# One output projection in a hybrid decoder step: pairs of full row tiles by seven half-size products in place of eight

## What is computed

```python
branch_a = jnp.einsum('blv,vd->bld', o_r.astype(dt), w_ret_up)
...
branch_b = jnp.einsum('blv,vd->bld', o_d.astype(dt), w_dn_up)

merged = jax.nn.sigmoid(gate_a) * branch_a + jax.nn.sigmoid(gate_b) * branch_b
h = h + jnp.einsum('bld,de->ble', merged, w_out)

u = rmsnorm(h, norm_ffn)
grp_logits = (jnp.einsum('bld,dg->blg', u, w_router_group) + b_router_group).astype(f32)
...
exp_logits = (jnp.einsum('bld,de->ble', u, w_router_expert) + b_router_expert).astype(f32)
...
w_top = jax.nn.softmax(top_v, axis=-1) * p_grp
```

## Time and profile before

| | us |
|---|---|
| median of three runs | 884.6 |
| lowest, highest | 884.51, 887.13 |
| the profiled execution's own time | 886.13 |
| its span in the trace | 884.3 |

### The profile page before, as it was taken

The page is one execution under the profiler, slowest core; times in us unless marked ns, Lnnn a source line. Parts: engine busy times, 40 slices in busy tenths (PEclk is TensorE's granted clock), DMA queues, the critical chain, the costliest instruction groups (busy, mean ns, idle before and its releaser), DMA issues.

```text
span 884.3 us, 11837 instructions
## 1 busy us (share of the span) xinstructions
PE 862.4 (98%) x4657; PEld 558.2 (63%) x4657; DVE 363.5 (41%) x833; ACT 223.4 (25%) x476; POOL 153.5 (17%) x186
## 2 busy tenths in 40 slices
PE   9999999999999999999999999999999999999996
PEld 4546777887799876776777755455444444444452
DVE  3223565766556325566434542234311111104553
ACT  2211243274223211131011103120211111125554
POOL 0324320022243314200300340002000000003100
PEclk9999999999999999999999999999999999999998
DMA  9512342502020202334122235015999999785111
GB/s 365 186 76 91 127 133 99 149 1 103 1 98 3 96 2 67 135 126 132 65 126 95 97 126 210 24 45 218 389 373 370 360 378 348 298 310 172 59 49 47
DMA packets 19813, 135.98 MB, mean 154 GB/s; under 512 B 2512, under 2 KB 3024, under 8 KB 12592
## 3 DMA queue, kind: packets, MB, share of 16 engines
q1 hardware_dynamic: 12176, 103.28, 30.5%
q0 software_dynamic: 5424, 26.45, 8.5%
q10 hardware_dynamic: 2160, 5.51, 2.1%
HBM read 117.83 MB, written 21.60 MB: 158 GB/s over the span
## 4 chain that ended last, share of the span: by engine, by line
PE 87%; DVE 4%; ACT 4%; issue 2%; DMA 1%; POOLq 0%; POOL 0%; ACTq 0%; DVEq 0%
PE pair L718 15%; PE single L1200 12%; PE single L898 11%; PE pair L1108 7%; PE pair L1189 6%; PE pair L793 4%; PE pair L769 3%; PE pair L1302 3%; PE pair L919 3%; PE single L919 3%; PE single L1177 2%; PE pair L1240 2%; PE single L974 1%; PE single L996 1%; PE single L993 1%
## 5 line engine op out<-in xcount | busy, mean ns | idle before, releaser
L718 PE MATMUL pair<-mem 128*128 128x288 f32 x640 | 158.9, 408 | 0.0
L718 PEld LDWEIGHTS pair<-mem 128*128 128x128 f32 x640 | 120.3, 190 | 35.6 <-ACT mem L1323 2.1
L1200 PE MATMUL single<-mem 128*128 128x512 f32 x256 | 112.8, 593 | 1.4 <-DVE mem L2160 1.4
L898 PE MATMUL single<-mem 128*128 128x288 f32 x448 | 110.1, 407 | 0.2
L898 PEld LDWEIGHTS single<-mem 128*128 128x128 f32 x448 | 84.7, 190 | 25.8 <-issue 1.6
L1200 PEld LDWEIGHTS single<-mem 128*128 128x128 f32 x256 | 47.3, 190 | 54.7 <-issue 53.1
L1323 ACT ACTIVATE mem<-single 128x256 f32<-128x256 f32 (+5 forms) x113 | 46.5, 421 | 132.7 <-PE single L1117 51.0
L1323 ACT ACTIVATE mem<-pair 128x512 f32<-128x512 f32 (+5 forms) x83 | 36.6, 492 | 162.5 <-PE pair L718 63.1
L1108 PE MATMUL pair<-mem 128*128 128x512 f32 (+1 forms) x192 | 64.6, 527 | 0.5 <-DVE mem L2000 0.5
L2153 DVE SCALAR_TENSOR_TENSOR mem<-single,mem 128x256 f32<-128x256 f32 x16 | 7.7, 484 | 138.8 <-PE single L1200 126.3
L1302 PE MATMUL pair<-mem 128*128 128x512 f32 (+1 forms) x192 | 63.4, 524 | 0.9 <-DVE mem L2206 0.9
(11 more groups left out here) (385 smaller groups left out, 1111.9 us busy)
## 6 DMA issues: line engine op xcount, KB each, us to landing
mem<-in_w_gu SPq DMA_DIRECT2D x16, 2048.0 KB, 9.5
mem<-in_w_down SPq DMA_DIRECT2D x16, 1024.0 KB, 11.8
y_slots<-mem SPq DMA_DIRECT2D x16, 512.0 KB, 3.9
y_slots<-in_zeros POOLq DMA_DIRECT2D x8, 512.0 KB, 8.1
mem<-in_w_ga SPq DMA_DIRECT2D x2, 2048.0 KB, 8.5
mem<-in_w_gb SPq DMA_DIRECT2D x2, 2048.0 KB, 8.4
mem<-in_w_wo SPq DMA_DIRECT2D x2, 2048.0 KB, 8.4
mem<-in_w_pg SPq DMA_DIRECT2D x2, 2048.0 KB, 11.3
```

The costliest lines, as they stand in the source:

```text
L718: last = nc.tensor.matmul(pb[:, hf, 0:HALF], w(k), rhs[:, k, hf * HALF:(hf + 1) * HALF], start=(k == 0), stop=(k == kk - 1))
L898: last = nc.tensor.matmul(single[plan.buf[s]][:, 0:HALF], lhs[:, k, :], rhs[:, k, :], start=(k == 0 and j in (0, 1, 3, 4)), stop=(k == 3), ...
L1200: last = nc.tensor.matmul(single[3][:, :], xT[u % 2][:, k, :], w_gu[u][:, k, :], start=(k == 0), stop=(k == KD - 1))
```

## The change

The four full tiles go in pairs, (0, 1) and (2, 3). Of a pair, the two row tiles, the two halves of the 1024 features and the two halves of the 1024 output columns make eight half-size products of four matmuls. The change replaces them by seven products on sums and differences of rows and weights (`sx`, with `sh` for the first half of the seventh), in the same scheme of sums that the branch groups have. The half with index h holds the feature blocks 2h, 2h+1, 4+2h and 5+2h.

- Weights: four combinations `sum_w`. Two are made by VectorE in steps of 512 columns behind products 1 to 4 of each of the last two branch groups (`sxT` 0 and 1), two of 2048 columns ahead of the first pair (`sxT` 2 and 3).
- Rows: four combinations for each pair (`sxS`), 512 columns each, with one more add; those of the first pair behind the last branch group, those of the second among the first pair's products.
- Results: ScalarE copies the first product of a pair from its bank; VectorE forms two partial sums (`sxu`), adds them to the residual rows (`sxp`) and then adds the banks (`wo`), ten adds of 512 columns per pair where there were four.
- Order: tiles now pass the router as 1, 0, 3, 2, 4 and the small tile is projected last, its two halves cut into four steps (`wg`, `wo`, `wh`, `wo`) among the router steps of tiles 3 and 2. The router steps of tiles 1 and 0 stand among the second pair's products.
- SyncE loads expert 1's weights after the sixth product of pair 1, as two of the weight sums lie in its place. GpSimd stores the rows of tiles 1 and 3 after their first half, which is now the later one.

The core of the diff:

```diff
-ORDER = [0, 4, 1, 2, 3]
+ORDER = [1, 0, 3, 2, 4]
...
+                if r == q == 1 and 0 < j < 5:
+                    out += [("sxT", x, j - 1)]
                 if r == q == x == 0:
                     out += {0: [("nf", "oN", 0)], 1: [("nf", "oN", 1)], 2: [("nf", "oN", 2)], 3: [("nf", "oN", 3)]}.get(j, [])
+        return out
+
+    def wo_pair(p, early):
+
+        out = []
+        for j in range(7):
+            out += early[j] + [("sx", p, j)]
+            out += {1: [("sxp", p, 0), ("wo", 2 * p, 0)] + [("sxS", 1, i) for i in range(3) if p == 0], 3: [("sxu", p), ("sxp", p, 1), ("sxp", p, 2)],
+                    4: [("wo", 2 * p + 1, 1)], 5: [("wo", 2 * p + 1, 0)], 6: [("wo", 2 * p, 1)]}.get(j, [])
         return out
 
     for r in range(2):
         for g in range(4 * r, 4 * r + 4):
             s += fast_group(g)
         s += fast_pair(r, 0) + fast_pair(r, 1)
-    for i, t in enumerate(ORDER):
-        s += [("wo", t, 0)]
-        if i: s += [("x2b", ORDER[i - 1])]
-        if i >= 2: s += [("rank", ORDER[i - 2])]
-        if i: s += [("rt", ORDER[i - 1])]
-        s += [("wh", t)]
-        if i: s += [("rtT", ORDER[i - 1])]
-        s += [("x2a", t), ("sqa", t)]
-        if i >= 2: s += [("ids", ORDER[i - 2])]
-        if i == 3: s += [("ovp", 0)]
-        s += [("wo", t, 1)]
-    y, z = ORDER[3:]
-    s += [("idv", t) for t in ORDER[:2]] + [("x2b", z), ("rank", y), ("rt", z), ("rtT", z), ("ids", y)]
+    s += wo_pair(0, [[("sxS", 0, 0), ("sxS", 0, 1), ("sxT", 2, 0), ("sxS", 0, 2), ("sxT", 3, 0)], [], [], [], [], [], [("sh", 0)]])
+    x2 = lambda t: [("x2a", t), ("sqa", t)]
+    s += wo_pair(1, [x2(1) + [("x2b", 1)], x2(0) + [("rt", 1)], [("x2b", 0), ("rtT", 1)], [("rt", 0)], [("rtT", 0), ("rank", 1)],
+                     [("ids", 1), ("rank", 0), ("ovp", 0)], [("sh", 1), ("ids", 0)] + x2(3) + [("x2b", 3)]])
+    s += [("wg", 4), ("rt", 3)] + x2(2) + [("wo", 4, 0), ("rtT", 3), ("x2b", 2), ("wh", 4), ("rt", 2), ("wo", 4, 1)] + x2(4)
+    s += [("rank", 3), ("rtT", 2), ("x2b", 4), ("idv", 1), ("ids", 3), ("rank", 2), ("rt", 4), ("idv", 0), ("ids", 2), ("rtT", 4)]
+    z = 4
...
+            if k == "sx":
+                nmm += 1
+                self.mm[s], self.before[s] = nmm, None
+            if k == "wo" and s[1] == 4:
+                nmm += 1
+                self.mm[s] = nmm
+                self.buf[s], self.before[s] = s[2], (None, ("wo", 3, 0))[s[2]]
+                last[("pair", s[2])] = s
...
+        half_rows = lambda t, h: mT.rearrange("p (a h b) c -> p a h b c", a=2, h=2)[:, :, h, :, t * P:t * P + P]
+        half_w = lambda i, h: ring[(13 + i) % RING].rearrange("p (a h r) -> p a h r", a=2, h=2)[:, :, h, :]
+        sum_w = [view(at, 2, 1024) for at in (OR, slot(0), UT + 2048, slot(4))]
+        sum_rows = [[view(at + 512 * i, 2, 2, P) for i in range(4)] for at in (RINGO + 2048, SQ)]
+        wpart = [view(slot(24 + i), 512) for i in range(3)]
...
+        sx_bank = [pair[i // 2][:, i % 2, :] for i in (0, 1, 2, 0, 3, 2, 3)]
...
+            free[1] = ("sx", 1, 5)
...
+                elif k0 in ("sx", "sh"):
+                    p = s[1]
+                    j = 6 if k0 == "sh" else s[2]
+                    ta, tb = 2 * p, 2 * p + 1
+                    prev = [("uy", 1, 1, 1, 2), ("uy", 1, 1, 1, 1), ("uy", 1, 1, 1, 5), None, ("uy", 1, 1, 1, 6), None, ("wo", tb, 1)] if p == 0 else \
+                           [None, ("wo", 0, 0), ("wo", 1, 0), None, ("wo", 0, 1), None, ("wo", tb, 1)]
+                    if prev[j] is not None:
+                        ev_wait(pe, prev[j])
+                    if j == 0 and p == 1:
+                        pe.wait_ge(sem("sx_part"), 1)
+                    if j == 3:
+                        pe.wait_ge(sem("sx_p0"), p + 1)
+                    if j == 5:
+                        pe.wait_ge(sem("sx_part"), 2 * p + 2)
+                    w_at = {0: (0, 0), 1: (0, 1), 6: (1, 1)}.get(j)
+                    if w_at:
+                        chunk(("wo", 4, w_at[0]))
+                    else:
+                        pe.wait_ge(sem("sum_w"), {2: 4, 3: 9, 4: 8, 5: 10}[j])
+                    if j in (2, 3, 4, 6):
+                        pe.wait_ge(sem("sum_rows"), 3 * p + {2: 1, 3: 2, 4: 2, 6: 3}[j])
+                    wgt = half_w(*w_at) if w_at else sum_w[{2: 2, 3: 1, 4: 0, 5: 3}[j]]
+                    rows = {0: half_rows(ta, 0), 1: half_rows(ta, 1), 5: half_rows(tb, 1)}[j] if j in (0, 1, 5) else \
+                        sum_rows[p][{2: 2, 3: 1, 4: 0, 6: 3}[j]]
+                    for i, (u, v) in enumerate([(1, 0), (1, 1), (0, 0), (0, 1)]):
+                        if j == 6 and (i < 2) != (k0 == "sh"):
+                            continue
+                        if p == 0 and j < 2 and i in (0, 2):
+                            if (j, i) != (0, 2):
+                                pe.wait_ge(sem("mT"), 4 if j == 0 else 6)
+                            if (j, i) == (1, 2):
+                                pe.wait_ge(sem("mTv"), 2)
+                        last = nc.tensor.matmul(sx_bank[j], rows[:, u, v, :], wgt[:, u, 512 * v:512 * v + 512],
+                                                start=(i == 0 and j < 5), stop=(i == 3), skip_group_check=True)
...
+                elif k0 == "sx" and s[2] == 0:
+                    mm_wait(act, s)
+                    if s[1]:
+                        act.wait_ge(sem("sx_pre"), 1)
+                        act.wait_ge(sem("sx_part"), 1)
+                    else:
+                        act.wait_ge(sem("mT"), 6)
+                        act.wait_ge(sem("mTv"), 2)
+                    copy(wpart[0], sx_bank[0]).then_inc(sem("sx_p0"), 1)
...
+                elif k0 == "sxT":
+
+                    _, i, c = s
+                    if i == 0 and c == 0:
+                        mm_wait(dve, ("wy", 7, 6))
+                        for n in (13, 14):
+                            dve.wait_ge(sem(f"ring{n % RING}"), 16 * (n // RING + (n % RING > 0)))
+                    to, plus, minus = [(sum_w[2], half_w(1, 1), half_w(1, 0)), (sum_w[0], half_w(1, 0), half_w(0, 0)),
+                                       (sum_w[1], half_w(1, 1), sum_w[0]), (sum_w[3], half_w(0, 1), sum_w[1])][i]
+                    if i < 2:
+                        to, plus, minus = (x[:, c // 2, 512 * (c % 2):512 * (c % 2) + 512] for x in (to, plus, minus))
+                    else:
+                        dve.wait_ge(sem("sum_w"), 6 + i)
+                    V.tensor_tensor(to, plus, minus, ALU.subtract).then_inc(sem("sum_w"), 1)
+                elif k0 == "sxS":
+
+                    _, p, i = s
+                    ta, tb = 2 * p, 2 * p + 1
+                    to = sum_rows[p]
+                    diff = lambda out, plus, minus: V.tensor_tensor(out, plus, minus, ALU.subtract)
+                    if i == 0:
+                        if p == 0:
+                            mm_wait(dve, ("uy", 1, 1, 1, 6))
+                            dve.wait_ge(sem("mT"), 6)
+                            dve.wait_ge(sem("mTv"), 2)
+                        diff(to[2], half_rows(ta, 0), half_rows(tb, 0)).then_inc(sem("sum_rows"), 1)
+                    elif i == 1:
+                        link(V.tensor_tensor(to[0], half_rows(tb, 0), half_rows(tb, 1), ALU.add))
+                        diff(to[1], to[0], half_rows(ta, 0)).then_inc(sem("sum_rows"), 1)
+                    else:
+                        dve.wait_ge(sem("sum_rows"), 3 * p + 2)
+                        diff(to[3], half_rows(ta, 1), to[1]).then_inc(sem("sum_rows"), 1)
+                elif k0 == "sxp":
+
+                    _, p, i = s
+                    ta, tb = 2 * p, 2 * p + 1
+                    add = lambda t, n, part: V.tensor_tensor(h2[:, t, n * 512:n * 512 + 512], h2[:, t, n * 512:n * 512 + 512], part, ALU.add)
+                    dve.wait_ge(sem("ld_h"), 16)
+                    if i == 0:
+                        dve.wait_ge(sem("sx_p0"), p + 1)
+                        add(ta, 0, wpart[0]).then_inc(sem("sx_pre"), 1)
+                    elif i == 1:
+                        dve.wait_ge(sem("sx_part"), 2 * p + 2)
+                        add(tb, 1, wpart[2]).then_inc(sem("sx_pre"), 1)
+                    else:
+                        add(tb, 0, wpart[1])
+                        add(ta, 1, wpart[1]).then_inc(sem("sx_pre"), 2)
+                elif k0 == "sxu":
+
+                    p = s[1]
+                    mm_wait(dve, ("sx", p, 3))
+                    dve.wait_ge(sem("sx_p0"), p + 1)
+                    if p:
+                        dve.wait_ge(sem("sx_pre"), 4)
+                    V.tensor_tensor(wpart[1], wpart[0], sx_bank[3], ALU.add).then_inc(sem("sx_part"), 1)
+                    dve.wait_ge(sem("sx_part"), 2 * p + 1)
+                    V.tensor_tensor(wpart[2], wpart[1], sx_bank[2], ALU.add).then_inc(sem("sx_part"), 1)
...
+                    if t < 4:
+                        p = t // 2
```

(33 more changed lines are left out.)

9 lines of the change are left out of this document (4 added, 5 removed).

## The result

The changed kernel takes **892.3 us** (median of 11 runs, 887.13 to 893.28) against 885.4 us for the kernel before (11 runs, 884.27 to 887.93, measured beside it): a ratio of 1.0054, 95% interval 1.0038 to 1.0071. It is slower by 0.5%, where 884.4 us and no measurable change were forecast, with 887.2 us as the upper end. The profiled execution of after took 892.34 us, its span is 890.6 us against 884.3.

A forecast was written before the change was run, and what follows sets the result against it. TensorE was taken as the bound; -6.9 + 3.1 + 0 + 2.8 + 2.1 - 0.8 = +0.3 us, but the queue walk's -0.2 was used: 884.6 - 0.2 = 884.4 us (50%, 882.5 to 886; 8 in 10: 880.6 to 887.2).

The forecast's parts named there:

- What bounds the kernel: Output projection and router, 519 to 602 us: TensorE carries the chain, busy 81.50 of 83 us; the last rtT step counts.
- What is removed: Projection: eight half-size products per pair of tiles become seven, 16 records fewer, 6.9 us of TensorE.
- First wait, the groups: Last two branch groups: GpSimd's lock delays VectorE's weight differences; TensorE loses 3.1 us at products 5, 6, then 5.
- the walk: Engine queues stepped through in the new order, projection and router: -0.2 us overall, taken as the forecast.
- Rival (a): Branch groups: the sums meet no GpSimd op, so the kernel is faster, 880.8 us; chance 22%.
- Second wait, the start of the pairs: Second product of pair 0 waits 0.5 us, replacing 0.5 at the first projection matmul: zero net.
- rival (c): Pair 0: VectorE becomes the bound, with a new wait before the sixth product; 886.8 to 888 us, chance 19%.
- Third, the ids step: ids step of pair 1: TensorE waits 2.8 us for VectorE's adds, router chain and pick.
- Fourth, the tail: After the last projection matmuls: waits of 0.4 at ids(3), 1.3 at rank(2), 0.4 at rank(4), together 2.1 us.
- The moved steps: GpSimd's row stores and SyncE's load of expert 1, now about 575 us, come in time for the gathered rows.
- the sum: All terms, branch groups to tail: -6.9 + 3.1 + 0 + 2.8 + 2.1 - 0.8 = +0.3 us.
- Rival (d): Projection and router stretch: slower because of TensorE's clock, with longest wait 2.8 us instead of 0.5; no size, chance 4%.

The follow-up runs named there:

- experiment 9: Experiment 4 with the eight weight differences placed again, seven among the last two branch groups' products, one ahead of the first row sum: 880.5 us, ratio 0.993.
- experiment 2: Changed kernel with three dummy products of 512 columns ahead of ids(1), in the wait: 891.1 us, ratio 1.0045.
- experiment 3: Changed kernel with a dummy product of 256 columns ahead of ids(3) and one of 512 ahead of rank(2): 887.6 us, ratio 1.0006.
- Experiment 4: Changed kernel with ids(1), rank(0), ovp one product later, ids(0) later, and two dummy products in the tail: 880.6 us, ratio 0.9926; run again 881.1 us, 0.9935.
- experiment 7: Kernel before with nine linked adds of 512 columns on VectorE, results unused, ahead of the pick of tile 1: 890.45 us, ratio 1.0052.
- experiment 5: Changed kernel with the eight weight differences in the last two branch groups cut from 512 to 8 columns: one execution, 886.4 us.
- experiment 6: Changed kernel with GpSimd's gate products and adds of the second branch cut to 8 columns: one execution, 888.95 us.

## Why the forecast was wrong, step by step

**What bounds the kernel: right.** TensorE carries the chain in every kernel; every microsecond that it lost or won between A and D came out of the end.

**What is removed: right.** 112 records of 128x512 stand in the projection for 128. 4641 records for 4657 in all; 6.9 us at full clock.

**First wait, the groups: right.** The lock between VectorE and GpSimd was there, in the groups and before the products that the walk named: 0.74 and 0.57 us of idleness before products 5 and 6, then 0.99 before 5. The list of waits adds up to 2.3, yet each costs 0.27 more, since four records take 1.24 us behind a wait and 0.97 in the flow (the groups of experiment 9 begin 6.79 us apart, seven times 0.97). Against experiment 9, where both groups run through, A to B is 16.69 − 13.58 = 3.1 us longer, and 3.1 was forecast. The first difference, issued at 506.30 with GpSimd's op of 505.97 under way, waited for about 1 us; the second only for 0.2. In the last group no difference waited at all, all four are like this one:

```profile
516.37 0.68 DVE L2083 TENSOR_TENSOR mem<-mem 128x512 f32<-128x512 f32 x1
```

There the two adds ahead of the group are held by GpSimd (1.09 and 1.84 us, from 513.12 and 514.24), so that its first evacuation comes late. Before has the same (1.84 at 513.62) and catches up, since nothing stands between its evacuations; the differences take that slack. The walk had the first of them caught by GpSimd instead: the same microsecond, by another path. Rival (a), the sums hidden, is refuted for this placing; experiment 9 shows that another placing does hide them.

**Second wait, the start of the pairs: 0.8 us too dear.** Before's wait of 0.5 us at its first projection product went (0.8 with what a wait adds), and none came for it: pair 0 runs without a gap, 56 records in 24.20 us. So neither the wait at its second product came nor one before its sixth, and rival (c), VectorE as the bound in pair 0, did not come either. Groups and start together: +2.3 for a forecast of +3.1.

**Third, the ids step: right as a wait.** 2.82 us against 2.8. VectorE's list is as walked: two linked adds, three adds, the router chain, the pick.

```profile
563.54 1.90 DVE L2106 TENSOR_TENSOR mem<-mem 128x512 f32<-128x512 f32 x3
...
568.09 0.48 DVE L2186 TENSOR_SCALAR mem<-mem,rj 128x128 f32<-128x128 f32 x2
```

**Fourth, the tail: 1.2 us against 2.1.** 0.41 at ids(3) (0.4 forecast), 0.83 at rank(2) (1.3), none at rank(4) (0.4). Before's 0.8 us of ScalarE waits went, as forecast.

**The moved steps: right.** SyncE's load of expert 1 starts at 576.49 (about 575 forecast), and no wait on it shows.

**The step that failed is the sum: it has no term for the clock.** The measured terms are −6.9 + 2.3 + 2.8 + 1.2 − 0.8 = −1.4 us, so on waits alone the kernel would have been a little faster than the forecast, which was −0.2. The trace says +7.5. The 8.9 us between them are products at half clock, and the experiments have it in two parts: the stretch behind the 2.8 us wait costs 3.2 us (experiment 2, from ids(1) to the small tile's first product), and the one in the tail 5.6 (after less experiment 3, A to D). Together 8.8, for 8.9 by the sum. (B to C of experiments 3 and 4 gives 77.15 − 70.85 = 6.3, less 2.8 of idleness 3.5; this holds what a wait adds to its idleness.) Experiment 4 checks the account from the other side. Its terms are −6.9 + 2.3 + 0.2 of wait + 1.2 − 0.8 = −4.0, with 1.2 for the tail's waits, which dummy work fills but does not shorten; A to D fell by 4.4 (101.4 to 97.0). These 0.4 us are not accounted for.

**Where I could have seen it.** Rival (d) names the very mechanism and the very wait, and then gives it 4% and no price. The row cited for it, a clock of 1.00 throughout the stretch, says only that waits of up to 0.5 us leave the clock alone; it says nothing of 2.8. The trace of before had rows that bear on it. Its waits of up to 1.5 us elsewhere leave the clock at 1.00 (the mean over the span is 0.997, and its last 6 us account for nearly all that is missing), but that is one execution and still short of 2.8; and at the very end, where TensorE has nothing left to do from 877.2 us on, the table by stretch of before reads:

```profile
876.00:878.00 2.00, 1.17 (x3) 0.19 (x1) 0.07 (x1) 0.77 (x2) 0.00 (x0) 1.00 0.00 0
878.00:880.00 2.00, 0.00 (x0) 0.00 (x0) 1.86 (x3) 1.96 (x4) 0.00 (x0) 0.81 0.00 0
880.00:884.00 4.00, 0.00 (x0) 0.00 (x0) 0.79 (x3) 1.18 (x4) 0.00 (x0) 0.50 0.35 131
```

Idle from 877.2, the clock is at 0.50 before 880: a wait of 2.8 us is as long as that. This row makes the rival a case to be priced, at the half-clock time of the products behind the wait, instead of 4% with no price. It does not make it certain, since other executions kept 1.00 for up to 5.3 us of idleness at their end (experiment 7). The fall came in all four profiles that have the 2.82 us wait (after, experiments 3, 5 and 6). The second stretch, behind two waits of 0.41 and 0.83 us, no row of before would have told.

The Trainium skill ("TensorE: Matmul & The Clock Gate", section "What's actually happening") has the throttled state as the default, which activity releases. The traces agree as far as they go: in experiment 2 dummy products without any use kept the clock at 1.00 at the ids step, and without work TensorE is at 0.50 at the end of every profile.

## What to carry to other kernels

Price a new wait of the bounding engine by its length and by what the engine does at the clock it has afterwards; look in the traces for the longest wait that left the clock at 1.00, and for the shortest idleness that did not, in more than one execution, since the same wait can do either. If an order of steps leaves a hole in TensorE's work that can't be closed, move the step first (here worth 6 us for one line), and fill what is left with dummy products that nothing waits for. Two engines that exclude each other for whole instructions are handled by placing the movable ones where the other engine is idle, read from the trace and read again after each move, since the moved work shifts the other engine's too.

## What the runs showed of the hardware

- TensorE's clock fell to half after a wait of 2.82 us, and after 2.55 us in the kernel before, and stayed there for about 6.8 us though the engine was busy without a gap (568.4 to 575.2); in the tail it stayed for about 13.6 us, with thin and dummy products, and in experiment 7 for about 3.4. Waits of up to 1.5 us in the profile of the kernel before left it alone; waits of 0.41 and 0.83 us, with 0.84 us of small router products between them, did not.
- Whether it falls differs between executions. Waits of 1.41 and 0.65 us in a branch group left it at 1.00 in the profiles of before and after and brought 0.50 for about 3.4 us in that of experiment 2; two of eight runs of experiment 7 (mean clock 0.999) can't have the stretch that its profile has; at the end of the twelve profiles it fell 2.1 to 5.3 us after the last product.
- The time at half clock differs between executions of one kernel: 0.986 to 0.993 in after's mean granted clock, 887 to 893 us. In the single execution of experiment 5 the tail's stretch lasted 6.8 us for 13.6 (C to D 11.0 us for 14.4).
- In the branch groups a wait costs 0.27 us more than the idleness that the list of waits shows (1.24 for 0.97 us of four records).
- A VectorE add or difference of two SBUF operands and a GpSimd multiply or add take turns by whole instructions even when GpSimd has its next one ready: 1.63, 0.92, 1.52 us for a difference of 0.68, and 1.24 for a GpSimd op of 0.80.
